# Multiplying the raw residual of norms 0, 2 and 3 in the next stage's first two tiles, and four weight buffers of 8 units in place of two of 12

## The reference

```python
for l in range(DEPTH):                       # DEPTH = 2
    x = layer_norm(ALPHA * x + 0.5 * swiglu(x, ffn1_w_in[l], ffn1_w_out[l]), ln1_g[l], ln1_b[l])   # norm 0
    mix = hybrid_mixer(x, mix_w_in[l], ..., mix_w_out[l])      # RG-LRU, gated linear attention, conv
    x = layer_norm(ALPHA * x + mix, ln2_g[l], ln2_b[l])                                            # norm 1
    x = layer_norm(ALPHA * x + memory_cross_attn(x, mem, xa_w_q[l], xa_w_kv[l], xa_w_o[l]),
                   ln3_g[l], ln3_b[l])                                                             # norm 2
    x = layer_norm(ALPHA * x + 0.5 * swiglu(x, ffn2_w_in[l], ffn2_w_out[l]), ln4_g[l], ln4_b[l])   # norm 3

def layer_norm(x, g, b):
    mu = mean(x); var = mean(square(x - mu))
    return (x - mu) * rsqrt(var + EPS) * g + b
def swiglu(x, w_in, w_out):                  # w_in: 1024 x 5632, w_out: 2816 x 1024
    gate, up = split(x @ w_in, 2)
    return (silu(gate) * up) @ w_out
```

## Time and profile before

| | |
|---|---|
| time, median of 3 runs | 2272.57 us (2271.89 to 2272.77) |
| the profiled execution's own time | 2275.68 us |
| its span, first to last instruction | 2273.9 us |
| TensorE (PE) busy | 2199.4 us, 97% of the span |
| VectorE (DVE) busy | 1044.4 us, 46% |
| ScalarE (ACT) busy | 783.4 us, 34% |
| GpSimd (POOL) busy | 998.8 us, 44% |
| mean granted TensorE clock | 0.991 of 2.4 GHz |
| data moved | 210.89 MB, mean 93 GB/s |

### The profile page before, as it was taken

The page is one execution under the profiler, slowest core; times in us unless marked ns, Lnnn a source line. Parts: engine busy times, 40 slices in busy tenths (PEclk is TensorE's granted clock), DMA queues, the critical chain, the costliest instruction groups (busy, mean ns, idle before and its releaser), DMA issues. The chain is left out here.

```text
span 2273.9 us, 26494 instructions
## 1 busy us (share of the span) xinstructions
PE 2199.4 (97%) x10932; PEld 1818.7 (80%) x10932; DVE 1044.4 (46%) x1108; ACT 783.4 (34%) x1066; POOL 998.8 (44%) x416
## 2 busy tenths in 40 slices
PE   7999999999999899999999999999999998999997
PEld 6888888788787788888878888887786887888886
DVE  2433234787735433332433332257877354333334
ACT  3322224735443422221333222246355334222223
POOL 5444444436432544444444444444265335444442
PEclk9999999999999999999999999999999999999999
DMA  4333322333322233332222333223243212333321
GB/s 165 100 95 96 111 99 56 86 101 103 111 84 65 66 100 95 96 114 92 72 91 93 102 96 114 87 65 84 84 118 105 83 65 70 98 94 101 111 90 50
DMA packets 96041, 210.89 MB, mean 93 GB/s; under 512 B 39344, under 2 KB 52016, under 8 KB 95664
## 3 DMA queue, kind: packets, MB, share of 16 engines
q1 hardware_dynamic: 93536, 205.55, 29.0%
q10 hardware_dynamic: 2384, 3.64, 0.5%
HBM read 207.06 MB, written 2.10 MB: 92 GB/s over the span
## 5 line engine op out<-in xcount | busy, mean ns | idle before, releaser
L468 POOL TENSOR_TENSOR w_lo<-raw,w_hi 128x1024 fp32r<-128x1024 f32 (+2 forms) x358 | 929.1, 2597 | 1228.2 <-ACT w_hi L1120 1228.0
L1120 ACT ACTIVATE w_hi<-raw 128x1024 fp32r<-128x1024 f32 (+2 forms) x358 | 401.5, 1122 | 1319.1 <-PE psum L553 1237.5
L547 PE MATMUL psum<-act_hi,w_hi 128*128 128x512 f32 x1840 | 726.1, 395 | 10.6 <-ACT w_hi L1120 4.1
L550 PE MATMUL psum<-act_lo,w_hi 128*128 128x512 f32 x1840 | 719.9, 391 | 0.0
L553 PE MATMUL psum<-act_hi,w_lo 128*128 128x512 f32 x1840 | 454.5, 389 | 0.0
L547 PEld LDWEIGHTS psum<-act_hi,w_hi 128*128 128x128 f32 x1840 | 347.6, 189 | 89.1 <-ACT w_hi L1120 4.7
L550 PEld LDWEIGHTS psum<-act_lo,w_hi 128*128 128x128 f32 x1840 | 347.8, 189 | 74.4 <-issue 2.4
L553 PEld LDWEIGHTS psum<-act_hi,w_lo 128*128 128x128 f32 x1840 | 345.3, 188 | 71.8
L1583 DVE TENSOR_TENSOR work<-work,psum 128x512 f32<-128x512 f32 x88 | 60.5, 688 | 611.4 <-PE psum L553 561.2
L547 PE MATMUL psum<-h_hi,w_hi 128*128 128x512 f32 x616 | 243.4, 395 | 0.0
L550 PE MATMUL psum<-h_lo,w_hi 128*128 128x512 f32 x616 | 243.1, 395 | 0.0
(11 more groups left out here) (250 smaller groups left out, 2130.3 us busy)
## 6 DMA issues: line engine op xcount, KB each, us to landing
raw<-w_in SPq DMA_DIRECT2D x176, 512.0 KB, 3.5
raw<-w_out SPq DMA_DIRECT2D x64, 704.0 KB, 4.0
raw<-w_kv SPq DMA_DIRECT2D x32, 512.0 KB, 3.5
raw<-w_mix SPq DMA_DIRECT2D x26, 512.0 KB, 3.6
raw<-w_q SPq DMA_DIRECT2D x16, 512.0 KB, 3.6
raw<-w_o SPq DMA_DIRECT2D x16, 512.0 KB, 3.5
raw<-w_v SPq DMA_DIRECT2D x4, 768.0 KB, 4.1
raw<-w_mix SPq DMA_DIRECT2D x24, 128.0 KB, 3.2
```

The costliest lines, as they stand in the source:

```text
L468: nc.gpsimd.tensor_tensor(w_lo[:, n % SPLIT, 0:width], raw[:, n % RAW, 0:width], w_hi[:, n % SPLIT, 0:width].bitcast(F32), ALU.subtract).t ...
L547: nc.tensor.matmul(o, hi, b_hi, start=start and k == 0, stop=False)
L550: nc.tensor.matmul(o, hi, b_lo, start=False, stop=False)
L1120: A(w_hi[:, n % SPLIT, 0:width], raw[:, n % RAW, 0:width], ACT.Copy).then_inc(w_hi_made, 1)
```

## The change

The change has three parts.

**Raw residual.** For norms 0, 2 and 3 (not the last norm of the last layer) the first two weight tiles of the next stage multiply z * gain, the residual before the norm, instead of the normed x. ACT writes its `hi` part (`raw_hi`) and DVE its `lo` part (`raw_lo`) after each residual tile, behind the squares. Two columns are appended to each row, gain and bias, so that rows have ROW = 514 elements (2056 bytes) and `act_hi`, `act_lo` become views of `acts_hi`, `acts_lo` with that row; half b of these products has 258 columns. The two extra columns give each output feature the sums that the norm needs: y = (W z' - mean * sum(W gain)) * scale + sum(W bias). ACT copies the two products out of PSUM (`sums_of`), DVE applies mean and scale (`normed_sums`). The next pair (`second_pair`) takes the normed x: its first tile by halves, its second whole.

**Where the normed x goes.** After norm 2 it goes to `act_hi`, `act_lo` (the raw parts are `z2_hi`, `z2_lo` in the shared region). After norms 0 and 3 the raw parts hold these, so the normed x goes to `x0_hi`, `x0_lo` or `x3_hi`, `x3_lo` in the shared region, and ACT copies it back with 8 copies of two tiles each (`returned`) before PE may go on to `k` 0 (mixer) or pair 3 (FFN).

**Weight buffers.** UNITS is 8 and SPLIT is 4. The FFN's second product is cut into three slots of 8, 7 and 7 units for each output tile (24 slots of 1024 or 896 columns for 16 of 1408), the mixer's values into 4 slots for 2. The load of `mem` moves from SP's queue to ACT's.

The core of the diff:

```diff
-UNITS = 12
-RAW, SPLIT = 4, 2
+UNITS = 8
+RAW, SPLIT = 4, 4
+OUT_UNITS = (0, 8, 15, 22)
+ROW = SEQ + 2
+RAW_NORMS = (0, 2, 3)
+def later(layer, n):
+    return n in RAW_NORMS and (layer, n) != (LAYERS - 1, 3)
-        act_hi = sb("act_hi", [P, KT, SEQ], F32R)
-        act_lo = sb("act_lo", [P, KT, SEQ], F32R)
+        acts_hi = sb("acts_hi", [P, KT, ROW], F32R)
+        acts_lo = sb("acts_lo", [P, KT, ROW], F32R)
...
+        act_hi, act_lo = acts_hi[:, :, 0:SEQ], acts_lo[:, :, 0:SEQ]
+        RAW_Z = {0: (acts_hi, acts_lo), 2: (z2_hi, z2_lo), 3: (acts_hi, acts_lo)}
+        NORMED = {0: (x0_hi, x0_lo), 1: (act_hi, act_lo), 2: (act_hi, act_lo), 3: (x3_hi, x3_lo)}
...
@@ gpsimd
             def after_norm(layer, s, x_layer, n):
                 split(layer, s)
-                split_x(x_layer, n, 0, 0)
                 split(layer, s + 1)
-                for h in range(2):
-                    for k in range(0 if h else 2, KT, 2):
-                        split_x(x_layer, n, h, k)
+                for k in range(0, KT, 2):
+                    split_x(x_layer, n, 0, k)
+                split(layer, s + 2)
+                for k in range(0, KT, 2):
+                    split_x(x_layer, n, 1, k)
+                split(layer, s + 3)
@@ tensor
-            def first_pair_by_halves(layer, s, x_layer, n):
...
+            def raw_pair(layer, s, x_layer, n):
+                z_hi, z_lo = RAW_Z[n]
+                def half(j, h, between=None):
+                    r = ring(layer, s + j)
+                    cols = slice(HALF, ROW) if h else HALVES[0]
+                    o = psum[:, 2 * j + h, 0:HALF + 2 * h]
+                    for k in range(KT):
+                        pe.wait_ge(raw_hi_made, raw_part(x_layer, n, k, h))
+                        nc.tensor.matmul(o, weight(r, k)[0], z_hi[:, k, cols], start=k == 0, stop=False)
+                        nc.tensor.matmul(o, weight(r, k)[1], z_hi[:, k, cols], start=False, stop=False)
+                        pe.wait_ge(raw_lo_made, raw_part(x_layer, n, k, h))
+                        last = nc.tensor.matmul(o, weight(r, k)[0], z_lo[:, k, cols],
+                                                start=False, stop=k == KT - 1)
+                        if between and k == 5:
+                            between()
+                    return last
+                slot_ready(layer, s)
+                half(0, 0, lambda: stats_rest(x_layer, n, 1))
+                half(0, 1).then_inc(slot_multiplied, 1)
+                slot_ready(layer, s + 1)
+                half(1, 0)
+                half(1, 1).then_inc(slot_multiplied, 1)
...
-                first_pair_by_halves(layer, S_MIX, layer, 0)
-                project("xa", 2)
-                project("cg", 0)
+                raw_pair(layer, S_MIX, layer, 0)
+                second_pair(layer, S_MIX + 2, [bank(0), bank(1)], layer, 0)
...
+                    if (kind, i) == ("k", 0):
+                        pe.wait_ge(x_returned, 2 * layer + 1)
@@ scalar
+            def scaled_later(layer, n, next_s, square_b, to):
...
+                def sums_of(j):
+                    act.wait_ge(slot_multiplied, next_s + j + 1)
+                    o = to(j)
+                    A(sums[:, 2 * j:2 * j + 2], psum[:, 2 * j + 1, HALF:HALF + 2], ACT.Copy)
+                    A(o[:, HALVES[0]], psum[:, 2 * j, HALVES[0]], ACT.Copy)
+                    A(o[:, HALVES[1]], psum[:, 2 * j + 1, HALVES[0]], ACT.Copy).then_inc(raw_sums_read, 1)
+                square_of_mean(layer, n, 0)
+                root(layer, n, 0)
+                if n != 2:
+                    w_hi_of(next_s + 1)
+                affines(0, 0)
+                affines(0, 2)
+                square_b()
+                w_hi_of(next_s + 2)
...
+                for k in range(0, KT, 2):
+                    affines(1, k)
+                    act.drain()
+                    copied(1, k)
+                    if k == 0:
+                        sums_of(0)
+                    if k == 4:
+                        w_hi_of(next_s + 3)
+                sums_of(1)
+                silu_table()
+            def returned(n, parts):
+                for part in parts:
+                    back, k = (act_hi, act_lo)[part // 4], part % 4 * 2
+                    last = A(back[:, k:k + 2, :], NORMED[n][part // 4][:, k:k + 2, :], ACT.Copy)
+                return last
...
@@ scalar, mixer
-                for t in range(AT):
-                    A(xa_pad[:, t, RG_K - 1:], read("xa", t), ACT.Copy).then_inc(evac, 1)
+                act.wait_ge(x_split, x_count(layer, 0, KT - 1, 1))
+                for s in range(2):
+                    step(layer, S_MIX + s)
+                returned(0, range(0, 4))
+                A(xa_pad[:, 2, RG_K - 1:], read("xa", 2), ACT.Copy).then_inc(evac, 1)
+                returned(0, range(4, 6))
                 A(CC[0], read("cg", 0), ACT.Sigmoid).then_inc(evac, 1)
+                returned(0, range(6, 8)).then_inc(x_returned, 1)
@@ vector
+                    if later(layer, n):
+                        raw_lo(layer, n, m, 0, slice(0, SEQ))
...
@@ vector, mixer
-                V.memset(SCORES[0], 0.0)
-                V.memset(SCORES[1], 0.0)
+                for t in range(2):
+                    to = xa_pad[:, t, RG_K - 1:]
+                    normed = normed_sums(layer, 0, t, to)
...
+                    V.tensor_scalar(to, to, sums[:, 2 * t + 1:2 * t + 2], None, ALU.add)
                 for t in range(AT):
                     short_conv(t)
                 gated_input(0)
+                dve.wait_ge(x_returned, 2 * layer + 1)
+                V.memset(SCORES[0], 0.0)
+                V.memset(SCORES[1], 0.0)
                 taps(0, 0, 24)
```

More of the change, by code:

```diff
@@ L397, in stage, with hidden_weights @@
                     load(dram, layer, s0 + i, first + i, per_layer or n)
+            def hidden_weights(dram, layer, s0):
+                half = FT // 2
+                for m in range(KT):
+                    for r in range(OUT_SLOTS):
+                        to, loaded = begin(layer, s0 + OUT_SLOTS * m + r)
+                        u0, u1 = OUT_UNITS[r:r + 2]
+                        for p in range(2):
+                            a, b = max(u0, p * half), min(u1, (p + 1) * half)
+                            if a < b:
+                                sp.dma_start(to[:, (a - u0) * P:(b - u0) * P],
+                                             rows(dram, (layer * KT + m) * 2 + p)[
+                                                 :, (a - p * half) * P:(b - p * half) * P]
+                                             ).then_inc(loaded, 16)
             def mix_tile(layer, kind, i):
@@ L820, in values @@
                     pe.wait_ge(gla_exp, layer * 2 + 2)
-                    for s in range(2):
-                        tokens_of(layer, S_MIX + V_SLOT + s, 4,
+                    for s in range(V_SLOTS):
+                        tokens_of(layer, S_MIX + V_SLOT + s, KT // V_SLOTS,
                                   [bank(4 + t, P, W_B) for t in range(TT)],
-                                  act_hi, act_lo, W_B, s * 4)
+                                  act_hi, act_lo, W_B, s * (KT // V_SLOTS))
                 def turned_keys():
@@ L1194, in ffn @@
                 s0 = layer * SLOTS + S_IN[f]
+                raw = norm_of(layer, f)
                 for i in range(FT):
+                    if raw and i == 0:
+                        act.wait_ge(raw_normed, raw_norm(*raw) + 1)
+                        A(work[:, 0, :], work[:, 0, :], ACT.Silu,
+                          bias=sums[:, 1:2]).then_inc(gate_silu, 1)
+                        for r in range(2):
+                            w_hi_of(s0 + r + SPLIT)
+                        continue
                     w_hi_of(s0 + 2 * i + SPLIT)
@@ L1198, in ffn @@
                         act.wait_ge(h_made, base + i - 1)
-                    A(work[:, i % 2, :], bank(2 * (i % 2)), ACT.Silu).then_inc(gate_silu, 1)
+                    if raw and not f and i == 1:
+                        act.wait_ge(x_split, x_count(*raw, KT - 1, 1))
+                        returned(3, range(0, 4))
+                    A(work[:, i % 2, :], bank(hidden_bank(layer, f, i, 0)),
+                      ACT.Silu).then_inc(gate_silu, 1)
                     w_hi_of(s0 + 2 * i + 1 + SPLIT)
+                    if raw and not f and i == 1:
+                        returned(3, range(4, 8)).then_inc(x_returned, 1)
                     if f == 0 and i in (4, 5):
@@ L1440, in attention @@
                     square(layer, 2, m, m, slice(0, SEQ))
-                square(layer, 2, KT - 2, KT - 2, HALVES[0])
-                square(layer, 2, KT - 1, KT - 1, HALVES[0])
+                    raw_hi(layer, 2, m, slice(0, SEQ))
+                for m in range(KT - 2, KT):
+                    square(layer, 2, m, m, HALVES[0])
+                    raw_hi(layer, 2, m, HALVES[0])
                 def square_b():
@@ L1565, in norm_by_halves @@
                         added_b()
```

(3 more changed lines are left out.)

415 lines of the change are left out of this document (263 added, 152 removed), and 2 rows, old and new, of the table MIX_STEPS.

## The result

| | before | after |
|---|---|---|
| time, median (lowest to highest) | 2272.67 us (2271.89 to 2273.09, 4 runs) | 2287.19 us (2286.26 to 2288.4, 4 runs) |
| ratio, 95% interval | | 1.0065 (1.0053 to 1.0078) |
| the profiled execution's own time, span | 2275.68, 2273.9 us | 2286.26, 2284.4 us |

The change makes the kernel 14.5 us slower. The forecast was 2267, its range ended at 2284.

A forecast was written before the change was run, and what follows sets the result against it. PE, 97% busy, plus its waits was taken to bound the kernel. Terms -9.7 - 5.4 - 6.0 - 3.1 + 1.1 + 17.3 = -5.8 us took the profiled 2275.68 to 2269.9; the median, 3.1 lower, gave 2267 us, range 2250 to 2284.

The forecast's parts named there:

- four buffers: Weight buffers: PE's waits for the third slot's copy after a first pair go, at three starts; -3.1 us in all.
- raw pairs, without the row price: Starts of stages behind norms 0, 2, 3: PE multiplies the raw residual instead of waiting; -9.7, -5.4, -6.0, with +1.1 for x0/x3.
- row price: 512-column matmuls on act_hi, act_lo: rows of 2056 bytes begin off multiples of 64, cost proportional to distance; +17.3 us.
- bounds of 4.3 and 30.2 us: Limits for slower 512-column steps: only tile k = 4 pays (4.3 us), or all of k = 1 to 7 (30.2 us).
- The rival of the full row price: Activation matmuls: every row not at a multiple of 64 bytes pays 0.0066 us; +7.1 us, 2280 us; chance 32%.
- the 1.1 us for `x0` and `x3`: Seven tiles reading x0 or x3 in the shared region pay 0.0066 us a matmul, as h does; +1.1 us.
- Norm 2: Boundary behind norm 2: the second pair's second tile ends 4.9 us sooner, twice; -9.7 us.
- Norm 3: Boundary behind norm 3, once: the pair ends at 1156.2 instead of 1163.2, next weight copy about 1157.0; -6.0 us.
- Norm 0: Boundary behind norm 0: pair ends 4.2 us sooner, 2.7 kept at the mixer's end because of DVE's taps, twice; -5.4 us.
- The third slot's wait: After a first pair, PE waits for a copy needing a buffer the pair holds (1.01 us idle); with four buffers it goes.
- The FFN's 24 slots for 16 hold the same matmuls: 0: FFN with the new weight buffers: more slots, same matmuls, so no change in time; 0 us.
- A PE that is done sooner waits longer: Stage behind norm 1: ACT sets its end, so fewer slot waits gain nothing; 0, at best -2 us a layer.

The follow-up runs named there:

- b_buffers: The kernel before with the change's four weight buffers of 8 units alone, no raw residual, rows 512 elements apart: 2274.72 us, ratio 1.001.
- a_pitch576: The changed kernel with activation rows 576 elements (2,304 bytes, 9 x 256) apart instead of 514: 2258.06 us, ratio to before 0.9936.
- b_rows514: The kernel before with only two unused elements behind each row of act_hi and act_lo (514 apart): 2301.76 us, ratio 1.013.
- a_pitch528: The changed kernel with rows of acts and z2 528 elements (2112 bytes) apart instead of 514: 2278.41 us, ratio to before 1.0024.
- b_region64: The kernel before with 32 unused bytes ahead of the shared region, which then begins at a multiple of 64: 2272.63 us, ratio 1.0.
- b_region256: The kernel before with 160 unused bytes ahead of the shared region, putting h, q and memory a multiple of 256 from the weights: 2257.15 us, ratio 0.993.
- a_early: The changed kernel, rows still 514, with a norm's last statistics issued after four of eight high passes, as before: 2281.14 us, ratio to before 1.0037.

## Why the prediction was wrong

The runs cut the 14.5 us into three steps, medians against medians:

| step | forecast | measured | from |
|---|---|---|---|
| four buffers | -3.1 | +2.4 | b_buffers, 2274.72 against 2272.28 |
| raw pairs, without the row price | -20.0 (-9.7 - 5.4 - 6.0 + 1.1) | -16.7 | a_pitch576, 2258.06 against 2274.72 |
| row price | +17.3 | +29.1 | 2287.19 against 2258.06 |
| sum | -5.8 | +14.8 | |

- **The step that failed is the size of the row price.** The term was rightly looked for: the step on `acts_hi` differs, and rows are the whole reason (b_rows514). But between bounds of 4.3 and 30.2 us the middle was taken, by a price in proportion to the distance from a multiple of 64 bytes. The criterion was wrong. The rows of before bore it, but also bore 256, since they held only distances of 0 and 96 (either way round); a_pitch528 and b_region64 refuted 64. Counted from a multiple of 256, rows of the change begin 128 to 184 bytes (`acts_hi`) and 192 to 248 (`acts_lo`) behind one. None is on it, so none is free, and together they pay 0.136 to 0.14 of the 0.16 us a tile that `h` and `q` pay: 8 steps took 1.85, against 1.83 for half and 1.86 for full. The text's own bound for wrong, a step more than 0.002 from 0.229, was passed: 5.580 / 24 = 0.2325.
- The rival of the full row price (2280, slower, 32%) had the direction and the size, 30.2 against 29.1, but the size in part by luck: it too counted from 64 bytes, and let one row in eight go free and seven pay 0.16 us a tile, where all eight pay 0.14 on the mean. It named the reason for doubt as well, "a step that costs for one odd offset may cost for all". What it missed, 7.2 us, is the rest: 5.5 for the buffers and 3.3 for the raw pairs, less 1.1 for the rows (medians of different batches leave half a us).
- The Trainium skill's sentence in "TensorE: Matmul & The Clock Gate", that two independent read ports make a weight load free for the running matmul, was put in doubt by 0.2336 against 0.226. b_region256 settles that much: the same matmuls over the same loads, 160 bytes on, lose 0.0067 us each. Whether the load or something else meets the moving rows was not tried. (By that sentence the 1.1 us for `x0` and `x3` would have gone too, so that the forecast's sum would be 18.4 us lower, not some 17.) The 16-byte cachelines of the Trainium skill's "SBUF — State Buffer", specifications, don't give the rule either: all starts in a_pitch528, and `h` everywhere, are multiples of 16, and pay.
- **Boundaries.** Norm 2: reckoned 4.9, measured 4.7, with another make-up: the wait at the statistics was 1.9 instead of 2.8, but the half clock did not go, against what the text expected (statistics 3.05 instead of 1.5 us). Norm 3 gave 7.1 for 6.0. Norm 0 gave 3.4 for 4.2 (PE waited 0.4 us at its statistics and 1.8 for half b's `x_hi`, which a_early cut to none and 0.5). But these gains mix the two parts of the change. By the same measure b_buffers stands at 31.1 and 31.2 (norm 0), 32.2 and 33.7 (norm 2) and 30.5 (norm 3), and a_pitch576 at 26.5, 28.3 and 28.0. So the buffers alone gave 3.8 of norm 3's 7.1 us and took 1.1 at norm 0, and the raw pairs gave 21.1 us at the five boundaries. Of these 16.7 arrived: up to 1.1 went to the steps on `x0` and `x3`, and the rest, 3.3 or a little more, is about what the forecast took as lost in the mixers (2 x 1.5); where it went was not traced.
- **Four buffers.** Alone they cost 2.4 us, with an interval of 0.2 to 4.3. The third slot's wait went as said. "The FFN's 24 slots for 16 hold the same matmuls: 0" failed: a slot's size also set where the statistics stand, which costs the change 6.1 us (a_early), 1.9 of them at the end, where no later stage can hide them. And the keys lost 1.5 to 1.7 us a layer through POOL's order, which the forecast did not lay out at all. "A PE that is done sooner waits longer" behind norm 1 held: it waits 7.0 us each time instead of 1.7, and goes on at most 0.3 us sooner.
- The forecast took the profiled execution to be 3.1 us above the median on both sides. After's lay 0.9 below its own. The median (14.5) and the spans (10.5) give differences that are 4 us apart.

## What to carry to other kernels

Before an fp32r kernel whose matmuls fill the span is tuned further, compare the step of its matmuls by operand pair (the chain shows them in one number), and try every moving tile at a multiple of 256 bytes from the weights, rows included: here padding alone was worth 15 us before the change and, as the sum of two runs, some 44 after it. When a change alters a row length or a tensor's size, price what it does to the addresses of everything declared behind it. When it alters the size of a slot, look for what is placed by slots, not only at what is in them. Where two criteria fit the rows at hand, price both; a middle between bounds belongs to neither.

## What was not expected of the hardware

- The step of a matmul with 512 columns in this format depends on the distance between its two operands in a partition, modulo 256 bytes: 0.2267 us at 0, 0.229 at 64, 0.2333 at 96, 0.2327 (`q`) to 0.2333 (`h`) at 128, 0.2337 where the moving row lies 8 to 64 short of a multiple (`acts_lo` after). Shifting both by 32 bytes changes nothing. With rows 2,112 bytes apart, which takes in 0, 64, 128 and 192, a tile's mean step is 5.527 / 24 = 0.2303.
- That the distance of 256 itself is free, and not only 512 or 2,048, is shown by b_region256, in which the region lies at an odd multiple of 256 from the weights.
- A DVE product of two SBUF operands, 0.68 us by itself, took 2.60 to 2.88 us when it began just behind the start of a 2.4 us POOL instruction: it ends some 0.55 us after POOL's, as 154 of 158 such products in the trace of before do.
